# Seven products for a third pair of K steps in an MLP product, with the join on ScalarE and accumulating transfers

## What is computed

```python
def sqrelu_mlp(x, w1, w2):                 # x: 256 x 2048, w1: 2048 x 8192, w2: 8192 x 2048
    return (jnp.square(jax.nn.relu(x @ w1)) @ w2).astype(x.dtype)

x = x + rmsnorm(sqrelu_mlp(rmsnorm(x, norm_g[i, 2]), w1, w2), norm_g[i, 3])
```

## Time and profile before

| | us |
|---|---|
| median of 3 runs | 1784.87 (1784.84 to 1785.13) |
| the profiled execution, its own time | 1784.87 |
| its span in the trace | 1783.2 |

### The profile page before, as it was taken

The page is one execution under the profiler, slowest core; times in us unless marked ns, Lnnn a source line. Parts: engine busy times, 40 slices in busy tenths (PEclk is TensorE's granted clock), DMA queues, the critical chain, the costliest instruction groups (busy, mean ns, idle before and its releaser), DMA issues.

```text
span 1783.2 us, 26260 instructions
## 1 busy us (share of the span) xinstructions
PE 1776.4 (100%) x8839; PEld 1507.5 (85%) x8839; DVE 1222.7 (69%) x1596; ACT 843.9 (47%) x1130; POOL 115.9 (6%) x162
## 2 busy tenths in 40 slices
PE   9999999999999999999999999999999999999999
PEld 7888888888888888888888887888888888888887
DVE  6567777556788778778877777755688655555654
ACT  7434444446444444445444455744444455543442
POOL 1012121000000000000000000100013011000000
PEclk9999999999999999999999999999999999999999
DMA  9664445555565556655655665555555555555554
GB/s 329 197 222 164 165 164 166 188 174 188 173 233 190 188 189 196 201 193 188 198 197 187 203 203 189 195 191 197 177 188 177 197 174 184 170 176 190 184 189 153
DMA packets 95078, 339.88 MB, mean 191 GB/s; under 512 B 11025, under 2 KB 11425, under 8 KB 94625
## 3 DMA queue, kind: packets, MB, share of 16 engines
q1 hardware_dynamic: 93392, 333.23, 56.7%
q0 software_dynamic: 752, 5.26, 0.8%
q10 hardware_dynamic: 864, 0.44, 0.1%
HBM read 336.77 MB, written 2.11 MB: 190 GB/s over the span
## 4 chain that ended last, share of the span: by engine, by line
PE 98%; DVE 1%; DMA 0%; ACT 0%; POOL 0%; SPq 0%; issue 0%; DVEq 0%
PE bank L458 41%; PE bank L437 23%; PE bank L442 12%; PE bank L751 6%; PE bank L750 6%; PE bank L752 6%; PE bank L474 1%; PE bank L508 1%; PE bank L587 1%; PE bank L628 1%; PE bank L643 1%; PE bank L634 0%; PE bank L627 0%; PE bank L644 0%; DMA gate<-in_x_turned 0%; PE bank L558 0%
## 5 line engine op out<-in xcount | busy, mean ns | idle before, releaser
L1387 DVE TENSOR_TENSOR w_lo<-raw,w_hi 128x1024 fp32r<-128x1024 f32 x620 | 757.4, 1226 | 439.6 <-ACT w_hi L932 435.3
L932 ACT ACTIVATE w_hi<-raw 128x1024 fp32r<-128x1024 f32 x620 | 651.9, 1057 | 658.7 <-PE bank L458 344.4
L458 PE MATMUL bank<-w_hi,h_both 128*128 128x512 f32 x1544 | 480.1, 392 | 0.0
L437 PE MATMUL bank<-h_both,w_hi 128*128 128x512 f32 x1792 | 432.7, 394 | 0.0
L437 PEld LDWEIGHTS bank<-h_both,w_hi 128*128 128x128 f32 x1792 | 330.7, 188 | 65.1
L458 PEld LDWEIGHTS bank<-w_hi,h_both 128*128 128x128 f32 x1544 | 288.0, 188 | 58.2
L458 PE MATMUL bank<-w_lo,h_both 128*128 128x512 f32 x772 | 301.2, 390 | 0.0
L442 PEld LDWEIGHTS bank<-h_both,w_lo 128*128 128x128 f32 x1792 | 229.8, 191 | 8.7
L442 PE MATMUL bank<-h_both,w_lo 128*128 128x256 f32 x1792 | 232.5, 283 | 0.0
L458 PE MATMUL bank<-w_hi,a_both 128*128 128x512 f32 x576 | 178.5, 391 | 0.0
L458 PEld LDWEIGHTS bank<-w_lo,h_both 128*128 128x128 f32 x772 | 145.0, 188 | 30.5
(11 more groups left out here) (232 smaller groups left out, 1210.3 us busy)
## 6 DMA issues: line engine op xcount, KB each, us to landing
raw<-in_stream SPq DMA_DIRECT2D x622, 512.0 KB, 3.4
res<-in_x SPq DMA_DIRECT2D x4, 512.0 KB, 7.2
rowg<-in_norm_rows POOLq DMA_DIRECT2D x2, 1024.0 KB, 8.4
gate<-cum_rows POOLq DMA_DIRECT2D x1, 2048.0 KB, 7.5
out<-wide SPq DMA_DIRECT2D x8, 256.0 KB, 4.8
gate<-in_x_turned SPq DMA_DIRECT2D x5, 256.0 KB, 6.5
raw<-in_stream SPq DMA_DIRECT2D x3, 256.0 KB, 5.1
gate<-in_x_turned SPq DMA_DIRECT2D x1, 512.0 KB, 7.3
```

What stands on the lines that cost most here:

```text
L437: pe.matmul(tile_sum[b][:, :], w_hi[:, slot + half, k * P:(k + 1) * P], h_both[:, 8 * half + k, :], start=half == 0 and k == 0, stop=False)
L458: mm = pe.matmul(dst[t][:, :], xt[:, k0 + 2 * j + k, tt], wt[:, slot, w], start=j == 0 and k == 0 and n == 0, stop=last and k == 1 and n == 2)
L932: nc.scalar.activation(w_hi[:, slot, :], raw[:, slot, :], ACT.Copy).then_inc(hi_ready, 1)
L1387: nc.vector.tensor_tensor(w_lo[:, slot, :], raw[:, slot, :], w_hi[:, slot, :].bitcast(F32), ALU.subtract).then_inc(lo_ready, 1)
```

## The change

- `SEVEN_PAIRS` gets a third pair and `SEVEN_AT` becomes (4, 8, 12); the order of pairs in the packed weights follows. Forms of the tokens get a third place; `x_form_lo` moves into the room of `rowg`.
- Of `join_seven` VectorE keeps the two sums `form_sum` and `form_sum2`. ScalarE copies P1, P5, P5, `form_sum` and `form_sum2` scaled by `rstd_sq` into five buffers (`addend`; three of them in the room of attention's bias, logit and prob).
- GpSimd adds them to the running sums by six accumulating DMAs per group, the second on (0,1) and on (1,1) after the first has landed (`added`).
- VectorE's plain drain of a place waits until the DMAs of that place have landed.
- TensorE waits at a group's start for the two sums and the first three scaled copies (`joined`), and at the first seven-product step for the plain drains.
- `rowg` is loaded after the last additions. Some semaphores elsewhere are merged.

```diff
-PAIR_ORDER = (0, 1, 4, 2, 3, 6, 5, 7)
-SEVEN_PAIRS = (4, 6)
-SEVEN_AT = (4, 10)
+PAIR_ORDER = (0, 1, 4, 2, 5, 3, 6, 7)
+SEVEN_PAIRS = (4, 5, 6)
+SEVEN_AT = (4, 8, 12)
+STEPS = len(SEVEN_AT)
...
+            def joined(w):
+                pe.wait_ge(join_step, 2 * w + 2)
+                pe.wait_ge(addend_ready, 5 * w + 3)
...
                 if w:
-                    pe.wait_ge(wide_taken, 2 * w - 1)
+                    joined(w - 1)
...
                     if j in SEVEN_AT:
                         if w:
-                            pe.wait_ge(wide_taken, 2 * w)
+                            pe.wait_ge(wide_taken, w)
...
-                    if j == SEVEN_AT[1] + 1:
-                        act.wait_ge(forms_done, 2 * w + 2)
-                        nc.scalar.activation(form_sum2, seven_bank[w % 2][0][:, :], ACT.Copy).then_inc(form_hi_ready, 1)
+                    if j == SEVEN_AT[-1] + 1:
+                        act.wait_ge(forms_done, STEPS * w + STEPS)
+                        nc.scalar.activation(form_sum2, p1, ACT.Copy).then_inc(form_hi_ready, 1)
+                        if w:
+                            act.wait_ge(added[0][0], 16 * w)
+                        nc.scalar.activation(addend[0], p1, ACT.Copy,
+                                             scale=rstd_sq[:, 0:1]).then_inc(addend_ready, 1)
+                        if w:
+                            act.wait_ge(added[0][1], 32 * w)
+                        nc.scalar.activation(addend[1], p5, ACT.Copy,
+                                             scale=rstd_sq[:, 0:1]).then_inc(addend_ready, 1)
+                        if w:
+                            act.wait_ge(added[1][1], 32 * w)
+                        nc.scalar.activation(addend[2], p5, ACT.Copy,
+                                             scale=rstd_sq[:, 1:2]).then_inc(addend_ready, 1)
+                        act.wait_ge(join_step, 2 * w + 1)
+                        nc.scalar.activation(addend[3], form_sum, ACT.Copy,
+                                             scale=rstd_sq[:, 0:1]).then_inc(addend_ready, 1)
+                        act.wait_ge(join_step, 2 * w + 2)
+                        if w:
+                            act.wait_ge(added[1][0], 16 * w)
+                        nc.scalar.activation(addend[4], form_sum2, ACT.Copy,
+                                             scale=rstd_sq[:, 1:2]).then_inc(addend_ready, 1)
...
+                dve.wait_ge(added[t][n], (32 if n else 16) * (w + 1))
                 add_scaled(w, t, n, plain_bank[w % 2][2 * t + n][:, :]).then_inc(ff_sum_ready, 1)
...
+            def join_seven(w):
+                p6, p7 = [seven_bank[w % 2][k][:, :] for k in range(2, 4)]
+                dve.wait_ge(form_hi_ready, (STEPS + 1) * w + STEPS + 1)
+                nc.vector.tensor_tensor(form_sum, form_sum2, p6, ALU.add).then_inc(join_step, 1)
+                dve.wait_ge(join_step, 2 * w + 1)
+                nc.vector.tensor_tensor(form_sum2, form_sum, p7, ALU.add).then_inc(join_step, 1)
...
+                for q, at in enumerate(SEVEN_AT):
+                    step = STEPS * w + q
+                    outer_sums(step, c + at, at % RING)
+                    inner_sum(step, at % RING)
+                    last_sum(step, at % RING)
+                    for k in range(2):
+                        rest(c + at - RING + k, (at + k) % RING)
+                        if q == 0 and n == 1:
+                            for half in range(2):
+                                plain_drain(w - 1, k, half)
+                    form_rest(step)
+                    for k in range(2, 4):
+                        rest(c + at - RING + k, (at + k) % RING)
+                rests(c + 12, range(2))
+                join_seven(w)
+                rests(c + 12, range(2, RING))
...
+            def add_up(w, t, n, src):
+                start = 1024 * (w % 2) + GROUP_COLS * n
+                pool.dma_start(group_sum[:, t, start:start + GROUP_COLS], src,
+                               accum_op=ALU.add).then_inc(added[t][n], 16)
...
+            for w in range(WIDE_GROUPS):
+                if w >= 2:
+                    pool.wait_ge(wide_taken, w - 1)
+                pool.wait_ge(addend_ready, 5 * w + 1)
+                add_up(w, 0, 0, addend[0])
+                pool.wait_ge(addend_ready, 5 * w + 2)
+                add_up(w, 0, 1, addend[1])
+                pool.wait_ge(addend_ready, 5 * w + 3)
+                add_up(w, 1, 1, addend[2])
+                pool.wait_ge(addend_ready, 5 * w + 5)
+                add_up(w, 1, 0, addend[4])
+                pool.wait_ge(added[0][1], 32 * w + 16)
+                add_up(w, 0, 1, addend[3])
+                pool.wait_ge(added[1][1], 32 * w + 16)
+                add_up(w, 1, 1, addend[4])
```

More of the change, by code:

```diff
@@ L178, in build @@
                             for name, at in (("form_hi", 3072), ("form_lo", 4608))]
-        x_form_hi, x_form_lo = [nc.alloc_sbuf_tensor_at(name, [P, 2, 4, P], F32R, offset=gate_base + 4 * at)
-                                for name, at in (("x_form_hi", 6144), ("x_form_lo", 7168))]
+        x_form_hi, x_form_lo = [nc.alloc_sbuf_tensor_at(name, [P, STEPS, 4, P], F32R, offset=at)
+                                for name, at in (("x_form_hi", gate_base + 4 * 6144), ("x_form_lo", rowg_base))]
+        scaled = nc.alloc_sbuf_tensor_at("scaled", [P, 3, GROUP_COLS], F32, offset=bias_base)
+        addend = [scaled[:, n, :] for n in range(3)] + [gate_flat[:, 7680:8192], rowg[:, 1536:2048]]
         form_sum2 = spare[:, 1024:1536]
@@ L319, in build @@
         wide_taken = sem("wide_taken")
+        addend_ready = sem("addend_ready")
+        added = [[sem(f"added{t}{n}") for n in range(2)] for t in range(NT)]
         head_relu = sem("head_relu")
@@ L782, in seven_products @@
                 slot = j % RING
-                first, last = q == 0, q == 1
+                first, last = q == 0, q == STEPS - 1
                 pe.wait_ge(lo_ready, c + j + 1)
                 product(seven[0], x_block(kt, 0), w_block(slot, 0), first, last)
-                pe.wait_ge(x_form_ready, 2 * g + q + 1)
+                pe.wait_ge(x_form_ready, STEPS * g + q + 1)
                 product(seven[1], x_form(q, 0), w_block(slot, 1), first, last).then_inc(chunk_done, 1)
@@ L1184, in wide_splits @@
                 w = 2 * g + n
+                p1, p5 = [seven_bank[w % 2][k][:, :] for k in range(2)]
                 for j in range(WIDE_CHUNKS):
@@ L1187, in wide_splits @@
                     if ahead in SEVEN_AT:
-                        act.wait_ge(form_step, 4 * (2 * w + SEVEN_AT.index(ahead)) + 2)
+                        act.wait_ge(form_step, 4 * (STEPS * w + SEVEN_AT.index(ahead)) + 2)
                     next_split(c + j)
                     if ahead - 1 in SEVEN_AT:
-                        step = 2 * w + SEVEN_AT.index(ahead - 1)
+                        step = STEPS * w + SEVEN_AT.index(ahead - 1)
                         act.wait_ge(form_step, 4 * step + 4)
@@ L1307, in _ @@
                     act.wait_ge(uz_scaled, g + 9)
-                    nc.scalar.activation(uz_a[b], uz_x[b], ACT.Tanh, scale=0.5).then_inc(zb_tanh, 1)
+                    nc.scalar.activation(uz_a[b], uz_x[b], ACT.Tanh, scale=0.5).then_inc(uz_tanh, 1)
                     split(c + 1, 2 * b + 1, lap)
@@ L1705, in x_forms @@
             def x_forms(g, q):
-                step = 4 * (2 * g + q)
+                step = 4 * (STEPS * g + q)
                 a11, a21 = [relu2[0][:, t * P:(t + 1) * P] for t in range(NT)]
@@ L1733, in outer_sums @@
                     dve.wait_ge(raw_landed[slot + s], 16 * (c // RING) + 16)
+                if step:
+                    dve.wait_ge(form_lo_ready, step)
                 b11, b12, b21, b22 = w_blocks(slot)
```

114 lines of the change are left out of this document (33 added, 81 removed).

## The result

The changed kernel takes **1819.6 us** (median of 4 runs, 1816.8 to 1821.0) against 1785.0 for the kernel before (4 runs): ratio 1.0192, 95% interval 1.0174 to 1.0209. It is slower by 34.6 us, far outside the scatter of either, where I had forecast faster by 4.8 and a range up to 1795. The profiled execution took 1819.83 us, with a span of 1818.1 against 1783.2 before.

The account below looks back on a forecast made before the run. TensorE, busy 1776.4 of 1783.2 us, was taken to bound the kernel. 21 products less save 4.76 us, with ScalarE, VectorE and the adding transfers costing no waits: 1784.87 - 4.76 = 1780.1 us, range 1779.2 to 1795.

Parts of the forecast that it names:

- The gain: Seven wide groups each turn one more pair into seven products: 21 products less at 0.2267 us, 4.76 us saved.
- ScalarE and VectorE: Their new order in the wide groups: VectorE 4.5 us gained against 4.5 lost, ScalarE six copies more, no wait of TensorE.
- R3: Rival: third step too soon for VectorE's forms in wide groups, up to 1 us each, 1782 to 1787; three rivals together 17%.
- The limits: Latest landings before TensorE waits: fifth by 7.05, sixth by 8.35 into tiles; fifth by 7.7, sixth by 10.1 into odd groups.
- T: Time in us counted from a wide group's end, where the next group's plain products start.
- The six places: Three passages from a group into the hidden tiles and three from an even into an odd group, where late additions reach TensorE.
- I take s = 1.3: Time in us one adding transfer holds its queue, bounds 1.0 to 2.6; some 30% of it allowed for the weight stream.
- The row nearest to it: Two 512 KB POOL transfers issued 0.6 us apart, the second landing 2.6 us behind the first; gave s its upper bound.
- the forecast's own formula: 3 x larger of (5s - 8.65), (6s - 9.95) at tile transitions plus 3 x larger of (5s - 9.3), (6s - 11.7) at odd groups.
- R1: Rival, 23% beyond s = 2.0: slow queue of additions makes TensorE wait; 1795 at s = 2.2, 1808.8 at 2.6.
- over 4 us to spare: Last wide group's drains, placed between remainders, were claimed to have this slack, so no wait there.

Follow-up runs that it names:

- no_adds: Changed kernel without the adding transfers of the first six wide groups and the waits for them (sums incomplete): 1781.4 us, ratio 0.998 to the kernel before.
- adds_aside: Changed kernel with the first six groups' adding transfers sent into spare buffers, drains not waiting (sums incomplete): 1781.6 us, ratio 0.9981 to the kernel before.
- dve_adds: Changed kernel with VectorE making the six additions itself right behind its two sums, no adding transfers, full computation: 1780.4 us, ratio 0.9975 to the kernel before.
- adds_after: Changed kernel with the first six groups' additions started after VectorE's plain drains, full computation: 1782.8 us, ratio 0.9988 to the kernel before.
- the lone one: Changed kernel keeping only the first adding transfer in each of the first six groups, first drain waiting for it (sums incomplete), one run: 1782.3 us.
- pool_adds: Changed kernel with GpSimd adding the scaled copies itself by tensor additions instead of transfers, full computation: 1788.8 us, ratio 1.0019 to the kernel before.
- half_after: Changed kernel with additions started after the drains only in odd groups 1, 3 and 5, full computation: 1800.0 us, ratio 1.0082 to the kernel before.

## Why the prediction was wrong, point by point

*The gain* was right: 8818 products, and 1784.9 - 1780.4 = 4.5 us with the additions on VectorE, against 4.76. In no_adds and adds_aside 3.5 and 3.4 came out. Most of the missing us lies behind the last wide group, whose six additions both keep: from 1044.5 to 1140 TensorE is idle for 1.2 us in no_adds and 2.1 in adds_aside, against 0.6 in dve_adds.

*ScalarE and VectorE* were laid out rightly: in dve_adds TensorE misses 0.24 of 558.5 us with more on VectorE than the change puts there. The third step does not come too soon (R3): the remainder of no form made TensorE wait.

*The limits* held. By the forecast VectorE must leave the drains by T = 9.05. At group 1 it left at 589.2, T = 12.3, so TensorE should wait 3.3 us; it waited 3.75. The six places are those named; a seventh, small one, lies behind the last wide group (below).

**The step that failed is "I take s = 1.3", with its "some 30% for the stream"**: the price of an adding transfer, 2.4 + 1.3 = 3.7 us. No row of an adding transfer stood behind it. It is right where the engines have room: 3.3 to 4.3 us for the first addition in adds_after, and 1.3 us between two landings where they are closest. But at a group's end the 16 engines are full (share 0.99 to 1.05 while the first addition is under way). There the first, with nothing before it in its queue, lands after 4.9 to 6.8 us (the lone one after 4.5 to 6.5, so company isn't needed for that), later ones come up to 4.5 us behind the one before, and the second round pays this again: at group 1 the fifth lands 6.9 us after its start, where I had 3.7.

How such a landing divides into a fixed part and a service time the runs don't settle. If the fixed part is left at 2.4 and the forecast's own formula is set equal to the 24.1 us of waiting, 3 x (6s - 9.95) + 3 x (6s - 11.7) = 24.1 gives s = 2.5, nearly twice what I chose and within the bounds. In the lone addition it would be 2.8, past them.

The row nearest to it was the pair of POOL transfers of the earlier trace rows, which spaced out by 2.6 us, and I set it aside because the engines were 91% busy there. In adds_aside they were full as well, with the additions themselves. I had reckoned with the load of before (62%) for a stretch that the change fills.

The Trainium skill, "DMA: Bandwidth & Descriptors", section "Anatomy of one DMA", gives 2.0 us + bytes / 436 GB/s, an estimated 2.6 us for 256 KB. The trace does not agree beside this stream: the first copies of a queue landed in 4.9 us and an addition in 5.2. The remark on two source reads, which the forecast places in Stop 4 of "Collectives: The Full Stack" of the Trainium skill, stands in that page's section "The bandwidth ceiling: the fold count and why AG ≠ RS ≠ AR"; the trace agrees with it, 1.3 us between landings for 0.6.

**What was in no case of mine is the clock.** R1 priced waits of TensorE at their length. With s = 2.6, 28.7 us of waits, it reached 1808.8. Measured are 24 us of waits and 13.1 us of slower products. Over the six places together a us of waiting cost another half, and this is why even the bound of the rival lay 11 us short. The rest is small: behind the last wide group, which was to have over 4 us to spare, the drains stood 5.9 us for the same fifth addition and TensorE waited 1.7 once in the plain group. The sum: 1778.4 forecast for the span, + 23.9 + 13.1 + 1.7 = 1817.1, against 1818.1.

*The chances.* R1 had 23%, and its places and its cause were right; its weight and its price were not, and its formula gives the waits only with an s of 2.5. A term on which six places hang and whose bounds are a factor 2.6 apart should not have taken a value near the low end.

## What to carry to other kernels

When work leaves an engine for a queue of transfers, ask who waits for the *last* of them and what stands behind that waiter. Two rounds on the same bytes are two landings in a row, and engines that were 62% busy before the change are full while it runs. Order can settle it: put the transfers behind the work that must not wait (1782.8 instead of 1819.6 us here), or leave six additions of 0.6 us on an engine that has 22% to spare (1780.4). Price a stall of TensorE by its length and by the slow products after it.

## What the runs showed of the hardware that was not expected

- *The clock at a wait.* At four of the six places the granted clock fell to 0.50 during the wait, at 592 about 0.7 us after the products had begun again. It stayed there for the first 3 to 6 us of products. These five waits were 3.1 to 5.4 us long. After the sixth, 3.01 us at 727.14, it stayed at 1.00. Together 13.1 us for 24 us of waiting. The Trainium skill, "TensorE: Matmul & The Clock Gate", "Part 1: The HAM clock gate (the "warmup" mystery)", says that a gap in the engine's work brings it back to half rate; the trace agrees at five places of six. The length of the wait alone doesn't tell: in pool_adds three waits of 2.0 us differ in it, the first with a fall and two without, and in half_after waits of 5.5 and 4.8 us have one and one of 2.8 has none. What decides is not settled by these runs.
- *Adding transfers.* 256 KB within SBUF: 5.2 us from start to landing alone at a group's end, 3.3 to 4.3 for the first behind the drains, 5.8 to 8.4 in a queue of six, against 4.7 to 5.3 for copies in that queue. Landings follow each other at 1.3 us at the least, copies at 0.6.
- *GpSimd beside VectorE.* An addition of 128x512 takes GpSimd 1.3 us on average in the first three of a group and 2.0 to 2.3 in the later ones, and VectorE's remainder beside it 1.60 to 1.84 us for 1.23. The Trainium skill, "SBUF — State Buffer", section "Who interferes with whom", says that a VectorE instruction with two inputs in SBUF contends with a GpSimd instruction that reads SBUF. The remainder has two such inputs (raw and w_hi), and the trace agrees. I had overlooked this when I expected 1780 to 1782 of pool_adds.
